# S5 tokens regrouped by copies on ScalarE and VectorE in place of products with the identity, a mixing order per layer, and the end in halves

## What is computed

```python
for l in range(DEPTH):                                    # DEPTH = 2
    x = layer_norm(ALPHA * x + 0.5 * swiglu(x, ...))      # 1024 -> 2816 -> 1024
    x = layer_norm(ALPHA * x + concat(a, b, c) @ w_out[l])
    x = layer_norm(ALPHA * x + memory_cross_attention(x, mem, ...))
    x = layer_norm(ALPHA * x + 0.5 * swiglu(x, ...))
# the three branches of the mix, all from proj = x @ w_in[l]
a = rms_norm(diff_attention(dq, dk, dv, lam), g)          # 4 heads, two softmax maps each
b = sigmoid(mo) * rms_norm(mlstm_chunkwise(mq, mk, mv, ig, lf), g)   # 4 heads
y = gelu(Re(C * scan(lam_bar, B * su)) + D * su)          # S5: 16 groups of 16 channels
c = y * sigmoid(y @ glu_w + glu_b)
```

## Time and profile before

| | us |
|---|---|
| median of 3 runs | 1301.18 (1300.43 to 1302.45) |
| profiled execution, its own time | 1304.04 |
| its span, first to last instruction | 1302.2 |
| TensorE busy | 1261.5 (97% of the span) |
| TensorE weight loads busy (beside it) | 1081.1 (83%) |
| VectorE busy | 767.0 (59%) |
| ScalarE busy | 590.1 (45%) |
| GpSimd busy | 161.8 (12%) |
| DMA | 219.46 MB, mean 169 GB/s |
| mean granted TensorE clock | 0.994 |

### The profile page before, as it was taken

One profiled execution on the slowest core, in us unless ns is written; L12 is line 12 of the kernel. 1 busy time (PEld: TensorE's weight loads), 2 busy tenths in 40 slices (PEclk: granted clock), 3 DMA queues, 4 the chain that ended last, 5 costly groups with the idle time before them and its releaser, 6 DMA issues.

```text
span 1302.2 us, 16434 instructions
## 1 busy us (share of the span) xinstructions
PE 1261.5 (97%) x6896; PEld 1081.1 (83%) x6896; DVE 767.0 (59%) x984; ACT 590.1 (45%) x671; POOL 161.8 (12%) x161
## 2 busy tenths in 40 slices
PE   7999999999999999999999999999998999999997
PEld 6888888897889888888888888888987897788885
DVE  5676746584545565454567676566746646644553
ACT  5444554446434544433444445544454444544341
POOL 1036700000111000000000068100001100000000
PEclk9999999999999999999999999999998999999999
DMA  9755554532356366555566655555232534655550
GB/s 331 246 194 175 180 175 149 162 98 68 112 194 193 128 200 208 181 188 193 195 194 194 194 194 173 183 162 164 83 108 72 190 129 136 205 182 189 194 192 34
DMA packets 160089, 219.46 MB, mean 169 GB/s; under 512 B 6896, under 2 KB 136048, under 8 KB 160016
## 3 DMA queue, kind: packets, MB, share of 16 engines
q1 hardware_dynamic: 156720, 206.60, 48.8%
q0 software_dynamic: 3152, 11.76, 2.7%
q10 hardware_dynamic: 144, 0.07, 0.0%
HBM read 217.34 MB, written 1.05 MB: 168 GB/s over the span
## 4 chain that ended last, share of the span: by engine, by line
PE 86%; DVE 5%; DMA 3%; ACT 3%; issue 1%; SPq 1%; POOL 0%; POOLq 0%; DVEq 0%; ACTq 0%
PE PS L508 26%; PE PS L510 26%; PE PS L509 26%; PE PS L539 1%; DVE WL L1534 1%; ACT WH L1132 1%; DMA RAW<-in_xattn_wkv 1%; PE PS L579 1%; SPq L397 1%; PE PS L1054 1%; PE PS L1078 1%; DMA RAW<-in_ffn_w_down 1%; PE PS L752 1%; DMA RAW<-in_w_out 1%; DMA RAW<-in_w_in 1%
## 5 line engine op out<-in xcount | busy, mean ns | idle before, releaser
L1534 DVE TENSOR_TENSOR WL<-RAW,WH 128x2048 fp32r<-128x2048 f32 (+1 forms) x199 | 447.9, 2255 | 271.4 <-ACT WH L1132 271.0
L1132 ACT ACTIVATE WH<-RAW 128x2048 fp32r<-128x2048 f32 (+1 forms) x199 | 370.6, 1871 | 173.1 <-DMA RAW<-in_ffn_w_up 120.4
L508 PE MATMUL PS<-WH,XH 128*128 128x512 f32 x768 | 307.2, 400 | 4.4 <-DVE WL L1534 2.3
L510 PE MATMUL PS<-WH,XL 128*128 128x512 f32 x768 | 300.7, 392 | 0.0
L509 PE MATMUL PS<-WL,XH 128*128 128x512 f32 x768 | 300.5, 391 | 0.0
L508 PEld LDWEIGHTS PS<-WH,XH 128*128 128x128 f32 x768 | 144.9, 189 | 36.4 <-issue 4.3
L510 PEld LDWEIGHTS PS<-WH,XL 128*128 128x128 f32 x768 | 144.7, 188 | 30.8
L509 PEld LDWEIGHTS PS<-WL,XH 128*128 128x128 f32 x768 | 145.0, 189 | 28.5 <-issue 0.5
L508 PE MATMUL PS<-WH,HH 128*128 128x512 f32 x352 | 137.5, 391 | 0.0
L510 PE MATMUL PS<-WH,HL 128*128 128x512 f32 x352 | 137.0, 389 | 0.0
L509 PE MATMUL PS<-WL,HH 128*128 128x512 f32 x352 | 137.0, 389 | 0.0
(11 more groups left out here) (318 smaller groups left out, 1739.8 us busy)
## 6 DMA issues: line engine op xcount, KB each, us to landing
RAW<-in_ffn_w_down SPq DMA_DIRECT2D x88, 512.0 KB, 4.4
RAW<-in_ffn_w_gate SPq DMA_DIRECT2D x87, 512.0 KB, 4.0
RAW<-in_ffn_w_up SPq DMA_DIRECT2D x87, 512.0 KB, 5.0
RAW<-in_w_in SPq DMA_DIRECT2D x44, 512.0 KB, 4.4
RAW<-in_xattn_wkv SPq DMA_DIRECT2D x32, 512.0 KB, 4.4
RAW<-in_xattn_wq SPq DMA_DIRECT2D x16, 512.0 KB, 4.1
RAW<-in_w_out SPq DMA_DIRECT2D x12, 512.0 KB, 4.4
RAW<-in_xattn_wo SPq DMA_DIRECT2D x12, 512.0 KB, 4.1
```

Of the source, the lines that this page charges most:

```text
L508: nc.tensor.matmul(out_ap, sh, mh, start=first, stop=False)
L510: return nc.tensor.matmul(out_ap, sl, mh, start=False, stop=last)
L1132: return nc.scalar.activation(dst, src, ACT.Copy)
L1534: return v.tensor_tensor(dst, full, hi.bitcast(F32), ALU.subtract)
```

## The change

The two regroupings leave TensorE. After ScalarE has written UT it makes U4 with 16 copies of 32 partitions by 2 x 64 elements (`stacked`, `in_order`), each onto other partitions, ahead of GATES; VectorE makes the way back with 16 such copies, ahead of `rope(3)`. ScalarE takes `diff_exp(0)` and `diff_exp(1)` ahead of a `split()`. TensorE takes `cols` behind the first tile of MM 1, and `turn_cat(0)` of layer 0 ahead of `mlstm_num`. In the middle of layer 1, which has no memory products, ScalarE and VectorE work in an order of their own. The last output unit W 4 is multiplied for tile 0 with its high parts first, and only then waits for the low part of the input; the first query unit waits by half tiles and takes its 32 products with the high part in each half first. At the end of layer 1 the last tile is finished in two halves of 512 columns: sum, scale and output DMA.

```diff
+        def stacked(tap, j):
+            return U4[32 * tap:32 * tap + 32, :, :].rearrange("c (f j) k -> c j f k", f=2)[:, j]
+        def in_order(tap, j):
+            return UT[32 * j:32 * j + 32, :, tap * STEPS:tap * STEPS + STEPS]
...
@@ TensorE, mix @@
                 mm.then_inc(gate_done.sem, 1)
-                s5_gather(l)
                 pe.wait_ge(roped.sem, roped.at(l, 1))
...
                 diff_scores(l, 1)
-                cols(l)
-
-                s5_scatter(l)
                 unit_ready(UNIT[l, "MM", 1])
                 form_a_tile(UNIT[l, "MM", 1], 1, 0, XH, XL, 0)
-                pe.wait_ge(ut_ready.sem, ut_ready.at(l, 2))
+                cols(l)
+                pe.wait_ge(g4_ready.sem, g4_ready.at(l, 1))
...
                 mlstm_scores(l, 3)
+                if FILL["mid", l]:
+                    pe.wait_ge(a_ready.sem, a_ready.at(l, 1))
+                    pe.wait_ge(do_read.sem, do_read.at(l, 3))
+                    turn_cat(l, CATA, 0, 5)
                 fill_read("mid", l, 1)
                 mlstm_num(l)
...
+                pe.wait_ge(cat_hi.sem, cat_hi.at(l, 3))
+                for i in range(2):
+                    for half in range(2):
+                        n = slice(512 * half, 512 * half + 512)
+                        nc.tensor.matmul(bank(half), CH[:, 2 + i, 0:P], wh[:, i, n], start=False, stop=False)
+                        nc.tensor.matmul(bank(half), CH[:, 2 + i, 0:P], wl[:, i, n], start=False, stop=False)
                 pe.wait_ge(cat_lo.sem, cat_lo.at(l, 3))
-                rows_product(UNIT[l, "W", 4], [2, 3], CH, CL, False, True)
...
@@ TensorE, end of the last FFN @@
+                if l + 1 == DEPTH and s == 1:
+                    rows_half(b + 31, [0, 1], HH, HL, 1, 0, False)
+                    h_turned(l, s, j + 1)
+                    unit_ready(b + 32)
+                    rows_tile(b + 32, [0, 1], HH2, HL2, 0, False, True).then_inc(y_half.sem, 1)
+                    rows_half(b + 31, [0, 1], HH, HL, 1, 1, False).then_inc(unit_used.sem, 1)
+                    rows_half(b + 32, [0, 1], HH2, HL2, 1, 0, True).then_inc(last_half.sem, 1)
+                    rows_half(b + 32, [0, 1], HH2, HL2, 1, 1, True).then_inc(unit_used.sem, 1)
+                    return
...
@@ ScalarE, mix @@
+                act.wait_ge(ut_ready.sem, ut_ready.at(l, 1))
+                for tap in range(TAPS):
+                    for j in range(BANDS):
+                        k = copy(stacked(tap, j), in_order(tap, j))
+                k.then_inc(u4_ready.sem, 1)
                 act.wait_ge(k_zero.sem, k_zero.at(l, 1))
                 evac(l, gate_done, 1, GATES[0:8, :], PS[0:8, 3, 0:SEQ], gate_tok)
-                act.wait_ge(u4_done.sem, u4_done.at(l, 1))
-                copy(U4[:, :, :], PS[:, 5, :].rearrange("p (i k) -> p i k", i=TILES)).then_inc(u4_ready.sem, 1)
                 split()
                 split()
                 conv_tap(l, 0)
-                split()
                 diff_exp(l, 0)
+                split()
                 diff_turned(l, 0)
...
                 diff_evac(l, 1)
+                if not FILL["mid", l]:
+                    diff_turned(l, 2)
                 act.wait_ge(c_hi_in.sem, c_hi_in.at(l, 1))
                 copy(CH[:, 6:8, :].rearrange("p f (k s) -> p f k s", s=TAPS),
                      UT[:, :, :].rearrange("p f (s k) -> p f k s", s=TAPS)).then_inc(c_hi.sem, 1)
-                split()
-                diff_turned(l, 2)
+                if FILL["mid", l]:
+                    split()
+                    diff_turned(l, 2)
...
@@ VectorE, mix @@
+                dve.wait_ge(gelu_done.sem, gelu_done.at(l, 1))
+                for tap in range(TAPS):
+                    for j in range(BANDS):
+                        k = v.tensor_copy(in_order(tap, j), stacked(tap, j))
+                k.then_inc(g4_ready.sem, 1)
+                rope(l, 3)
                 mid_split(l, 2)
-                rope(l, 3)
-                split()
                 diff_max(l, 1)
+                split()
...
+                else:
+                    decay_scores(l, 0)
+                    decay_scores(l, 1)
+                    diff_stats(l, 0)
+                    diff_sums(l, 2)
+                    diff_combine(l, 2)
+                    decay_scores(l, 2)
+                    decay_scores(l, 3)
+                    diff_max(l, 3)
+                    diff_norm(l, 0)
+                    c_low(l)
+                    mlstm_sums(l)
+                    cat_low(l, 0, 0, 5)
+                    diff_sums(l, 3)
+                    split()
+                    mlstm_scale(l)
+                    split()
+                    cat_low(l, 1, 4, 5)
```

More of the change, by code:

```diff
@@ L495, in _ @@
             out_v = out.rearrange("b (t p) d -> p (b t) d", p=P)
[L496 to L499, removed]
+            for i, (t, cols) in enumerate(((0, slice(0, D)), (1, slice(0, 512)), (1, slice(512, D)))):
+                sp.wait_ge(end_ready.sem, i + 1)
+                sp.dma_start(out_v[:, t, cols], X[:, t, cols]).then_inc(out_done.sem, 16)
+            sp.wait_ge(out_done.sem, 48)
         @block.tensor
@@ L553, in rows_tile, with rows_half @@
                                   first and i == 0, last and i == n - 1)
+                return mm
+            def rows_half(u, chunks, ah, al, t, half, last):
+                n = len(chunks)
+                wh = WH[u % RING][:, 0:n * D].rearrange("p (c n) -> p c n", c=n)
+                wl = WL[u % RING][:, 0:n * D].rearrange("p (c n) -> p c n", c=n)
+                tok = slice(t * P, t * P + P)
+                cols = slice(512 * half, 512 * half + 512)
+                for i, c in enumerate(chunks):
+                    mm = prod(bank(2 * t + half), ah[:, c, tok], al[:, c, tok], wh[:, i, cols], wl[:, i, cols],
+                              False, last and i == n - 1)
                 return mm
@@ L712, in form_b, with first_query @@
                 form_b_half(u, b, mh, ml, 1).then_inc(unit_used.sem, 1)
+            def first_query(l):
+                u = UNIT[l, "WQ", 0]
+                unit_ready(u)
+                wh = WH[u % RING][:, :].rearrange("p (c n) -> p c n", c=KC)
+                wl = WL[u % RING][:, :].rearrange("p (c n) -> p c n", c=KC)
+                for half in range(2):
+                    cs = range(4 * half, 4 * half + 4)
+                    pe.wait_ge(xT_hi.sem, xT_hi.at(l, 4 * 2 + 2 + half + 1))
+                    for c in cs:
+                        for f in range(2):
+                            o, cols = PS[:, 4, f * SEQ:f * SEQ + SEQ], slice(f * P, f * P + P)
+                            nc.tensor.matmul(o, wh[:, c, cols], XH[:, c, :], start=(c == 0 and f == 0), stop=False,
+                                             skip_group_check=True)
+                            nc.tensor.matmul(o, wl[:, c, cols], XH[:, c, :], start=False, stop=False,
+                                             skip_group_check=True)
+                    pe.wait_ge(xT_lo.sem, xT_lo.at(l, 4 * 2 + 2 + half + 1))
+                    for c in cs:
+                        for f in range(2):
+                            o, cols = PS[:, 4, f * SEQ:f * SEQ + SEQ], slice(f * P, f * P + P)
+                            mm = nc.tensor.matmul(o, wh[:, c, cols], XL[:, c, :], start=False, stop=(c == KC - 1),
+                                                  skip_group_check=True)
+                mm.then_inc(unit_used.sem, 1)
             def form_a_tile(u, half, b, ah, al, t):
@@ L1381, in mix @@
                 conv_tap(l, 0)
+                diff_exp(l, 0)
                 split()
-                diff_exp(l, 0)
                 diff_turned(l, 0)
@@ L1404, in mix @@
                 nc.scalar.activation(COUT[:, 2:4, :], COUT[:, 2:4, :], ACT.Silu).then_inc(silu_done.sem, 1)
+                diff_exp(l, 1)
                 split()
[L1406 to L1409, removed]
-                copy(UT[:, :, :], PS[:, 2, :].rearrange("p (f n) -> p f n", f=2)).then_inc(ut_ready.sem, 1)
                 act.wait_ge(glu_done.sem, glu_done.at(l, 1))
@@ L1621, in boundary @@
                 norm_var(l, n, 0)
+                if n == 3 and l + 1 == DEPTH:
+                    end(l, last)
+                    return
                 if n == 1:
```

127 lines of the change are left out of this document (78 added, 49 removed).

## The result

The changed kernel took 1288.93 us (median, 1288.46 to 1289.93), the kernel before 1301.82 beside it: a ratio of 0.9903 (95% interval 0.9885 to 0.992), 12.9 us or 1.0% faster. Run again beside the experiments it took 1288.67, ratio 0.9892 (0.9876 to 0.9909). The forecast was 1286.8, with 1281.0 to 1292.5 as its range. The profiled execution has a span of 1288.1, where 1287.8 was forecast, and an own time of 1289.93.

A forecast was written before the change was run, and what follows sets the result against it. TensorE, busy 97% of the span, was taken as the bound. Gains summed to 17.75 us, less 3.4 for the clock behind two new waits: 14.4, a span of 1287.8 and a median of 1286.8; range 1281.0 to 1292.5.

The forecast's parts named there:

- gather, layer 0: Late ScalarE splits make diff_turn(0) 0.89 us later, and a clock fall behind its wait costs 1.7: -2.6 us together.
- scatter, layer 0, without the gather's delay: VectorE copies replace 3.98 us of TensorE and end the wait at cols; 3.05 us gained net of the gather's 0.89.
- layer 0 from `diff_turn(1)` to W 4, without W 4's own: Layer 0's turn_cat(0) goes into a wait ahead of mlstm_num: 0.35 us gained.
- layer 1, first `mlstm_scores` to W 0: Layer 1's new order shortens two waits by 2.1 us each and avoids a 3.4 us clock fall; taken as 8.0.
- W 4, both layers: The last mixing unit starts with its high part, 0.7 us earlier in each layer: 1.4 us.
- first query, both layers: The first query starts when the first XH copy is done: 1.37 us in each layer, 2.75 in all.
- part 1: The gather in each layer, moved to ScalarE: TensorE's 2.39 us not saved, it waits at diff_turn(0); -2.6 us each.
- (a): Rival: the clock holds over the 3.5 us wait at diff_turn(0), giving 1283.4 us; chance 0.17.
- (b): Rival: the ScalarE gather copies overlap, 0.21 us each, giving 1283.6 us with the clock falls, 1280.2 without; chance 0.12.
- (c): Rival: layer 1's order only moves waits without the clock's gain, layer 0's diff_turn(1) wait brings a fall: 1291.9; chance 0.19.
- (d): Rival: copies onto other partitions cost much more; at 0.85 us per ScalarE copy the time is 1304; chance 0.02.
- (e): Rival: TensorE waits all the 2.39 us for U4 and layer 1's waits stay, giving 1297 us; chance 0.06.

The follow-up runs named there:

- gather_pe: Changed kernel with the gather alone put back on TensorE (16 products, one ScalarE copy out of PSUM): 1283.38 us, ratio 0.9863 to the kernel before.
- gather_dve: Changed kernel with the 16 gather copies on VectorE, behind rope(1), instead of ScalarE: 1278.36 us, ratio 0.9824 to the kernel before.
- max0_alone: Changed kernel with one move: diff_max(0) between the two s5_states on VectorE, gather still on ScalarE: 1279.19 us, ratio 0.9823 to the kernel before.
- mid_old: Changed kernel with the whole middle of both layers in the old order on VectorE, ScalarE and TensorE: 1294.44 us, ratio 0.9939 to the kernel before.
- scatter_pe: Changed kernel with the scatter put back on TensorE and the orders around it as before: 1294.31 us, ratio 0.9944 to the kernel before.
- late_waits: Changed kernel with the waits at W 4 and the first query undone, each waiting for its whole input: 1290.49 us, ratio 0.9911 to the kernel before.
- best1: Changed kernel with gather on VectorE, diff_max(0) between the s5_states, and diff_max(1) ahead of the third memory unit's split (first layer): 1274.17 us, ratio 0.9786.

## Why the prediction came out as it did

The span was forecast at 1287.8 and is 1288.1. So near a hit is luck in part: the terms that came out too small and those that came out too large are each over 2 us and cancel. I follow TensorE's starts in the two profiled executions, before less after; the changed kernel is 0.3 ahead already at the start of the mix.

| step | forecast | measured |
|---|---|---|
| gather, layer 0 | -2.6 | -2.5 (1.0 later, 1.5 clock) |
| gather, layer 1 | -2.6 | -3.5 (1.0 later, 2.5 clock) |
| scatter, layer 0, without the gather's delay | 3.9 | 3.9 |
| scatter, layer 1, likewise | 2.4 | 2.4 |
| layer 0 from `diff_turn(1)` to W 4, without W 4's own | 0.35 | 2.2 |
| layer 1, first `mlstm_scores` to W 0 | 8.0 | 7.5 |
| W 4, both layers | 1.4 | 1.2 |
| first query, both layers | 2.75 | 1.95 |
| end | 0.7 | 1.0 |

With the 0.3 at the start and -0.3 between the query and the last feed-forward part the right-hand column makes 14.1, the difference of the spans (1302.2 and 1288.1). Against the forecast, layer 0's middle brought 1.85 more, the end 0.3 more; layer 1's gather cost 0.9 more, and layer 1's middle, W 4 and the query brought 0.5, 0.2 and 0.8 less.

**Right:** the mechanism of part 1 (work off TensorE that is not saved, because the maximum is late and TensorE stands still), with the copy's price (0.31 forecast, 0.319), the wait at `s5_in` (0.6, 0.70), the splits 0.89 later (1.0, against the start of UT), the wait at `diff_turn(0)` (3.4 to 3.5, 3.30) and the fall behind it. gather_pe, gather_dve and max0_alone show this, and not only the trace; what the prediction did not look at is whether the maximum could stand earlier in VectorE's queue. The scatter's copies were 0.235 forecast and are 0.231; the new wait at `diff_turn(1)` 2 and is 1.79.

**Wrong in size:** the clock behind `diff_turn(0)`. I carried 1.7 over from rows 3 as a fixed price. The runs show 0, 1.5 or 2.5 behind the same wait of 3.3; the profiled execution paid 4.0 for the two together where the sum had 3.4. In the middle of layer 1 the two waits were priced right (4.2 forecast, 3.9 without the clock: 2.43 and 2.67 against 0 and 0.73, less the new 0.46), but the 3.4 of clock is the price in one execution; mid_old paid 1.7. The three terms make 7.6, and the 0.4 between them and the 8.0 of the sum has no row behind it; 7.5 was measured. The query was put at 1.37 in each layer (its own two times, 1041.08 and 1039.65, are 1.43 apart). It starts 1.3 earlier, but 0.3 of W 4's gain is lost on the way to it, at the transposes: 0.97 is left. Layer 0's `turn_cat` was too small: I counted the 0.35 that it fills, and left out the numerators' wait (1.04 to 0.38, by the order of `diff_max(3)` and `decay_scores`, which stands in both layers), the wait at `diff_turn(3)` (1.29 to 0.71) and the one of 0.69 behind it, which goes.

**Wrong in the reckoning:** "the same savings are taken from each", the step from the span to the median. The profiled execution of before was 2.9 slower than its median, that of the changed kernel 1.0. The medians are 12.9 apart, the profiled executions 14.1. That the falls of the clock cost more in that execution than in the median one fits (the same fall varied by 1.0 and 1.7 between kernels), but this is argued. The mean granted clocks of the 31 other executions of before, 0.992 to 0.997 around its 0.994, bear it out only loosely: the two fastest (1299.41 and 1299.68) have the 0.997, but one of 1303.74 has 0.995 and one of 1300.28 has 0.994.

**The rivals.** (a) The clock holds: no. Seven profiled executions, of six kernels, have the wait of 3.3 in both layers; the clock fell behind 13 of the 14, by 1.5 us in eight and by 2.5 in five. (b) The copies overlap: no, 0.319 at a distance. The Trainium skill, ScalarE: Activation LUTs, What ACT_TABLE_LOAD costs, has 186 ns plus 0.833 ns an element and about 93 ns of overlap for back-to-back copies, which makes 0.2 us each, an estimate; the trace has 0.319, and the measurement decides. (c) The order in layer 1 only moves the waits: no, they went, and so did the fall, and none followed the new wait of 1.79 in layer 0. (d) Dear copies onto other partitions: no, 0.319 and 0.231. (e) No: TensorE waits 0.7 for U4.

**The parts do not add up.** Undone one at a time they make -5.3 + 5.6 + 5.8 + 1.8 + 0.6 = 8.5 us, and the whole change 12.9. In the profiled executions, by spans, they make -6.4 + 3.7 + 4.9 + 1.7 + 1.1 = 5.0, and the whole change 14.1. What the profiles show of this gap of 9.1 is clock: in scatter_pe the fall behind `cols` that before had is missing (1.6), in mid_old the fall in layer 1's middle costs 1.7 in place of 3.4, in both the one behind layer 1's `diff_turn(0)` costs 1.5 in place of 2.5, and late_waits lacks one of 2.5 and has another of 1.6. That is 1.6 + 1.7 + 2 x 1.0 + 0.9 = 6.2 of the 9.1. The medians hold such falls too, but a profile shows those of one execution only, so how much of their gap of 4.4 is clock is not known. Nor was every piece undone by itself: `diff_exp(0)` ahead of a `split()` stands in all of these kernels.

## What to carry to other kernels

Work taken off the bounding engine pays only if what is queued behind its new place is not on the way to that engine's next wait: look at which engine is idle at that time (VectorE, for 9.3 us), not at which has the lower share over the span. Where a short step that the bounding engine needs stands behind long ones that it does not need yet, move the short one first; here one such move was worth 9.5 us, with no work removed. Undo each part of a bundle by itself, and then try the order around it: this one contained a loss of 5.3 us inside a gain of 12.9, and one moved step took it away.

## What the runs showed of the hardware

The price of a wait for the clock is no fixed number. Waits of 3.3 at the same place were followed by falls that cost 1.5 us (eight times), 2.5 (five) and nothing (once). A wait of 2.06 ahead of `cols` was followed by no fall, where one of 1.94 had one that cost 1.6; the wait of 2.4 in layer 1's middle by a clock of 0.53 in one kernel and of 1.00 in another; one of 0.74 by a clock of 0.66. None followed the waits of 1.8 at `diff_turn(1)`. What decides it is open: no run here varied it alone. It shows in the spread too: the four kernels whose waits in the mix are all under 2 us have runs within 0.3 us (max0_alone), 1.4 (gather_dve), 1.6 (best1) and 1.9 (gather_pe), those with waits of 3.3 within 1.5 to 3.8, and the kernel before within 3.1 to 6.3 beside the experiments. (Those are ranges of 4 to 6 executions, of the kernel before 9 to 11, and a range grows with their number.) The four of max0_alone all have a mean granted clock of 0.998 or 0.999.

A copy of 32 partitions by 128 float32 elements costs 0.319 us on ScalarE and 0.231 on VectorE, from SBUF to SBUF and mostly onto other partitions; on VectorE the direction makes no difference (gather 3.70 / 16, scatter 3.47 / 15).
